# Three 256-wide matmuls per weight tile in one 256-wide PSUM region, and one VectorE pass per block

## The reference

```
a = rmsnorm(h);  proj = a @ w_in                       # 2048 x 6790
h = h + concat(hgrn2(proj), fox(proj), moba(proj)) @ w_out
c = rmsnorm(h);  h = h + (gelu(conv3(c @ w_gate)) * (c @ w_up)) @ w_down    # 5632 wide
e = rmsnorm(h);  h = h + sigmoid(e @ w_ple_gate) * (p @ w_ple_proj)
# second block; scale, shift and gates from silu(c_2) @ w_mod_2
h = mod(rmsnorm(x)); proj = h @ w_in_2                 # sliding-window heads and latent (MLA) heads
x = x + g1 * (mix @ w_out_2)
x = x + g2 * (relu(h @ w_ff1_2)**2 @ w_ff2_2)          # 8192 wide
out = rmsnorm(x)
```

## Time and profile before

| | |
|---|---|
| median of 3 runs | 2540.63 us (2538.52 to 2541.36) |
| profiled execution, first to last instruction | 2547.7 us |
| PE busy | 2419.6 us (95%), 13460 matmuls |
| PEld busy | 2057.7 us (81%) |
| DVE busy | 1946.2 us (76%), 3035 instructions |
| ACT busy | 1092.2 us (43%) |
| mean granted TensorE clock | 0.980 |
| HBM read | 509 MB, 202 GB/s over the span |

### The profile page before, as it was taken

The page is one execution under the profiler, slowest core; times in us unless marked ns, Lnnn a source line. Parts: engine busy times, 40 slices in busy tenths (PEclk is TensorE's granted clock), DMA queues, the critical chain, the costliest instruction groups (busy, mean ns, idle before and its releaser), DMA issues.

```text
span 2547.7 us, 37180 instructions
## 1 busy us (share of the span) xinstructions
PE 2419.6 (95%) x13460; PEld 2057.7 (81%) x13460; DVE 1946.2 (76%) x3035; ACT 1092.2 (43%) x1472; POOL 115.0 (5%) x221
## 2 busy tenths in 40 slices
PE   6979999989999999999988989899899999999997
PEld 5868787878888888888877867778788888888886
DVE  4688677779998989898976756676777777777775
ACT  4334444444434344444345444644444344334432
POOL 0100000000000000000000010000000000000000
PEclk8989999999999999999999989999999999999999
DMA  5754466357887878778864544334355555545552
GB/s 198 270 186 149 154 225 215 139 196 261 286 289 266 284 260 281 273 277 284 277 214 153 207 161 159 116 102 162 134 187 193 183 183 187 193 169 193 185 183 82
DMA packets 86666, 516.76 MB, mean 203 GB/s; under 512 B 9861, under 2 KB 10389, under 8 KB 37360
## 3 DMA queue, kind: packets, MB, share of 16 engines
q1 hardware_dynamic: 57168, 407.93, 44.8%
q0 software_dynamic: 29200, 106.31, 12.4%
q10 hardware_dynamic: 144, 0.26, 0.0%
HBM read 509.22 MB, written 5.24 MB: 202 GB/s over the span
## 4 chain that ended last, share of the span: by engine, by line
PE 86%; DVE 8%; ACT 3%; DMA 2%; issue 2%; SPq 0%; DVEq 0%; POOLq 0%; ACTq 0%
PE ps L464 47%; PE ps L465 24%; PE ps L462 5%; PE ps L461 2%; PE ps L482 2%; DMA modraw<-in_wmod 2%; PE ps L532 1%; DVE wl L1147 1%; DVE yn L1246 1%; ACT wh L776 1%; PE ps L541 1%; DVE modraw L1200 1%; PE ps L580 1%; DVE xs L1233 1%; PE ps L550 0%
## 5 line engine op out<-in xcount | busy, mean ns | idle before, releaser
L464 PE MATMUL ps<-xs,wh 128*128 128x512 f32 x4003 | 1462.6, 406 | 41.5 <-DVE xs L1233 17.3
L776 ACT ACTIVATE wh<-raw 128x1024 fp32r<-128x1024 f32 x768 | 809.9, 1058 | 1077.6 <-PE ps L462 810.1
L1147 DVE TENSOR_TENSOR wl<-raw,wh 128x1024 fp32r<-128x1024 f32 x768 | 937.3, 1222 | 317.7 <-ACT wh L776 301.6
L465 PE MATMUL ps<-xs,wl 128*128 128x256 f32 x4003 | 1131.5, 283 | 0.0
L464 PEld LDWEIGHTS ps<-xs,wh 128*128 128x128 f32 x4003 | 761.0, 190 | 242.4 <-issue 42.4
L465 PEld LDWEIGHTS ps<-xs,wl 128*128 128x128 f32 x4003 | 766.0, 191 | 11.3
L464 PE MATMUL ps<-hs,wh 128*128 128x512 f32 x1504 | 543.5, 400 | 5.7 <-DVE hs L1506 3.3
L465 PE MATMUL ps<-hs,wl 128*128 128x256 f32 x1504 | 423.1, 281 | 0.0
L464 PEld LDWEIGHTS ps<-hs,wh 128*128 128x128 f32 x1504 | 284.2, 189 | 65.4 <-DVE hs L1506 3.6
L465 PEld LDWEIGHTS ps<-hs,wl 128*128 128x128 f32 x1504 | 285.5, 190 | 10.0
L1200 DVE CUSTOM_DVE_ANT_0 modraw<-modraw,cb 128x1024 f32<-128x1024 f32 x192 | 233.4, 1218 | 24.8 <-DMA modraw<-in_wmod 24.6
(11 more groups left out here) (210 smaller groups left out, 1493.8 us busy)
## 6 DMA issues: line engine op xcount, KB each, us to landing
raw<-in_w SPq DMA_DIRECT2D x384, 1024.0 KB, 4.9
modraw<-in_wmod POOLq DMA_DIRECT2D x192, 512.0 KB, 4.3
rel_rows<-rrow POOLq DMA_DIRECT2D x4, 768.0 KB, 3.9
x<-in_x SPq DMA_DIRECT2D x4, 512.0 KB, 6.1
tbias<-rel_rows POOLq DMA_DIRECT2D x16, 128.0 KB, 2.8
out_dram<-mix SPq DMA_DIRECT2D x4, 512.0 KB, 2.6
hmask<-in_hmask SPq DMA_DIRECT2D x1, 512.0 KB, 17.3
mix<-in_p ACTq DMA_DIRECT2D x1, 256.0 KB, 4.2
```

Source lines behind the costliest of these rows:

```text
L464: nc.tensor.matmul(out[:, :], hi[:, w], pair, start=s, stop=e)
L465: m = nc.tensor.matmul(out[:, 0:T], lo[:, w], src[:, k, 0, :], start=False, stop=e, skip_group_check=e)
L776: nc.scalar.activation(wh[:, h % HS, :], raw[:, u % RAW, (h % 2) * 1024:(h % 2 + 1) * 1024], ACT.Copy).then_inc(s_round, 1)
L1147: nc.vector.tensor_tensor(wl[:, h % HS, :], raw[:, (h // 2) % RAW, (h % 2) * 1024:(h % 2 + 1) * 1024], wh[:, h % HS, :].bitcast(F32), ALU. ...
```

## The change

Every tile is now done as the joined units did it: three matmuls of 256 columns, hi·hi, hi·lo and lo·hi, all into columns 0 to 255 of the bank. The 512-column form, the turned order at the end of a block and the argument `joined` are gone. `take` becomes a copy of 256 columns, and `add_blocks` one instruction per block, without the `link` between two.

```
-                            pair = src[:, k, :, :].rearrange("p a t -> p (a t)")
-                            if joined:
-                                ...
-                            elif e and not s:
-                                nc.tensor.matmul(out[:, 0:T], lo[:, w], src[:, k, 0, :], start=False, stop=False)
-                                m = nc.tensor.matmul(out[:, :], hi[:, w], pair, start=False, stop=True)
-                            else:
-                                nc.tensor.matmul(out[:, :], hi[:, w], pair, start=s, stop=e)
-                                m = nc.tensor.matmul(out[:, 0:T], lo[:, w], src[:, k, 0, :], start=False,
-                                                     stop=e, skip_group_check=e)
+                            nc.tensor.matmul(out[:, 0:T], hi[:, w], src[:, k, 0, :], start=s, stop=False)
+                            nc.tensor.matmul(out[:, 0:T], hi[:, w], src[:, k, 1, :], start=False, stop=False)
+                            m = nc.tensor.matmul(out[:, 0:T], lo[:, w], src[:, k, 0, :], start=False, stop=e)
...
-                nc.vector.tensor_reduce(dst, bank()[:, :].rearrange("p (a t) -> p t a", a=2), AX.X, ALU.add
-                                        ).then_inc(s_evac, 1)
+                nc.vector.tensor_copy(dst, bank()[:, 0:T]).then_inc(s_evac, 1)
...
-                bs = [bank() for _ in ks]
-                for q in range(2):
-                    ...
-                    if q == 0:
-                        link(*ins)
+                for k in ks:
+                    b = bank()[:, 0:T]
+                    if gate is None:
+                        m = nc.vector.tensor_tensor(x[:, k, :], b, x[:, k, :], ALU.add)
                     else:
-                        for i in ins:
-                            i.then_inc(s_evac, 1)
+                        m = nc.vector.scalar_tensor_tensor(x[:, k, :], b, gate[:, k:k + 1], x[:, k, :], ALU.mult, ALU.add)
+                    m.then_inc(s_evac, 1)
```

More of the change, by code:

```diff
@@ L433, in _, with unit @@
             c = Counts(pe, h=0, b=0, hp=0)
-            def unit(kind, src, xwait=None, between=None, joined=False):
+            def unit(kind, src, xwait=None, between=None):
                 for half in range(2):
@@ L454, in unit @@
                             s, e = first and n == 0, last and n == len(tiles) - 1
-                            pair = src[:, k, :, :].rearrange("p a t -> p (a t)")
-                            if joined:
-                                nc.tensor.matmul(out[:, 0:T], hi[:, w], src[:, k, 0, :], start=s, stop=False)
-                                nc.tensor.matmul(out[:, 0:T], hi[:, w], src[:, k, 1, :], start=False, stop=False)
-                                m = nc.tensor.matmul(out[:, 0:T], lo[:, w], src[:, k, 0, :], start=False, stop=e)
-                            elif e and not s:
-                                nc.tensor.matmul(out[:, 0:T], lo[:, w], src[:, k, 0, :], start=False, stop=False)
-                                m = nc.tensor.matmul(out[:, :], hi[:, w], pair, start=False, stop=True)
-                            else:
-                                nc.tensor.matmul(out[:, :], hi[:, w], pair, start=s, stop=e)
-                                m = nc.tensor.matmul(out[:, 0:T], lo[:, w], src[:, k, 0, :], start=False,
-                                                     stop=e, skip_group_check=e)
+                            nc.tensor.matmul(out[:, 0:T], hi[:, w], src[:, k, 0, :], start=s, stop=False)
+                            nc.tensor.matmul(out[:, 0:T], hi[:, w], src[:, k, 1, :], start=False, stop=False)
+                            m = nc.tensor.matmul(out[:, 0:T], lo[:, w], src[:, k, 0, :], start=False, stop=e)
                     m.then_inc(s_used, 1)
@@ L680, in _ @@
             for j in range(U_PLEP):
-                unit("oct", xs, XS["p"] if j == 0 else None, joined=True)
+                unit("oct", xs, XS["p"] if j == 0 else None)
             square_sums(N_PLE, 2)
@@ L722, in _ @@
             for u in range(U_UQ):
-                unit("uq", xs, XS["cq"] if u == 0 else None, lambda q: swa(2 * (U_IN2 + u) + q), True)
+                unit("uq", xs, XS["cq"] if u == 0 else None, lambda q: swa(2 * (U_IN2 + u) + q))
             pe.wait_ge(s_xs, XS["cq"] + 4)
             for u in range(U_UKV):
-                unit("one", xs[:, 3:4, :, :], between=lambda q: swa(2 * (U_IN2 + U_UQ + u) + q), joined=True)
+                unit("one", xs[:, 3:4, :, :], between=lambda q: swa(2 * (U_IN2 + U_UQ + u) + q))
             def mla(i):
@@ L1170, in take @@
             def take(dst):
-                nc.vector.tensor_reduce(dst, bank()[:, :].rearrange("p (a t) -> p t a", a=2), AX.X, ALU.add
-                                        ).then_inc(s_evac, 1)
+                nc.vector.tensor_copy(dst, bank()[:, 0:T]).then_inc(s_evac, 1)
             def add_blocks(ks, gate=None):
-                bs = [bank() for _ in ks]
-                for q in range(2):
[L1179 to L1185, removed]
-                    if q == 0:
-                        link(*ins)
-                    else:
-                        for i in ins:
-                            i.then_inc(s_evac, 1)
+                for k in ks:
+                    b = bank()[:, 0:T]
+                    if gate is None:
+                        m = nc.vector.tensor_tensor(x[:, k, :], b, x[:, k, :], ALU.add)
+                    else:
+                        m = nc.vector.scalar_tensor_tensor(x[:, k, :], b, gate[:, k:k + 1], x[:, k, :], ALU.mult, ALU.add)
+                    m.then_inc(s_evac, 1)
             def mods(n, where=None):
@@ L1547, in _ @@
             MODS, M0 = 3 * CH, c.n["m"]
-            c.loop(NC1 - 1, ffn1_body, h=6 * CH, b=2 * CH + KB, c=KB + 2 * CH + 2, m=MODS, g=CH, y=CH, l=CH)
+            c.loop(NC1 - 1, ffn1_body, h=6 * CH, b=2 * CH + KB, c=2 * CH + 2, m=MODS, g=CH, y=CH, l=CH)
             units(CH_LAST, conv, first=lambda: product(CH - 1),
@@ L1667, in ffn2_body @@
                     units(CH, relu2, first=last_down(G2), h_lo_of=lambda j: h_lo(q, j))
-            c.loop(NC2 // 2 - 1, ffn2_body, h=8 * CH, b=2 * (CH + KB), c=2 * KB, y=2 * CH, l=2 * CH)
+            c.loop(NC2 // 2 - 1, ffn2_body, h=8 * CH, b=2 * (CH + KB), y=2 * CH, l=2 * CH)
             downs(lambda: relu2(CH - 1), lo_first=lambda: h_lo(1, CH - 1), gate=G2)
```

## The result

| | before | after |
|---|---|---|
| median | 2539.72 us (4 runs, 2538.52 to 2541.36) | 2610.42 us (4 runs, 2602.39 to 2612.8) |
| profiled execution, span | 2547.7 us | 2600.7 us |
| ratio of the runs | | 1.0273, 95% interval 1.0256 to 1.0289 |

The change costs 71 us; +34 was forecast, and the range ended at 2604. The two traces differ by only 53 us, because the profiled execution of before is longer than any of its four runs and that of after is the shortest of its four.

What follows compares the result with a forecast made beforehand. The prediction took the kernel to be bound by PE's stream of matmuls, priced by the distance between starts. Its terms, +42 (PE) - 1 (hidden) - 7 (DVE) = +34 us, gave 2575 us, range 2546 to 2604.

Steps and rivals of the forecast that it cites:

- PE, 120 ns a matmul, +42: PE's matmul stream: three 256-column matmuls at 120.0 ns replace a tile of about 353 ns, together +42 us.
- the end of the joined runs and not their beginning: Joined units: 120.0 ns a step from the ninth step on was taken, not 117.5 in the first 8 steps.
- The Trainium skill's rule on the busy share of LDWEIGHTS: PE's weight loads as the measure of headroom: would cost some 1300 us more; given no weight.
- The distance rule of N/2.4 + 2.5 ns: Distance between PE matmul starts: the third matmul would cost 2.5 ns a tile, +15 us; set aside against the rows.
- What hides, -1: From 70 to 145 us, some 12 full units: slower PE fills idle time while DVE is held by modulation weight loads, -1 us.
- Register operations in the loops, 0: Half boundaries of the two FFN loops, 384 halves: taken as nothing, upper bound 0.12 us each, +46 us.
- rival 3: FFN loop half boundaries become visible, 0.03 to 0.12 us each, +12 to +46: 2587 to 2621 us; chance 0.15.
- DVE, -7: DVE loses some 190 us of busy time, but only PE's waits count: -7 us, between 0 and -12.
- the two waits of L464 for `up`: PE waits counted among three for a take; those and four for `wl` save 0.27 each, 2 us.
- Sum, +34: Whole kernel: +42 - 1 - 7 = +34 us, giving 2575 us on the runs' median.
- Elsewhere in the stream nothing hides it: PE's stream outside 70 to 145 us: the slower matmul pace counts in full, with no further deduction.

Runs made afterwards that it cites:

- e6: Changed kernel with hi·lo put into columns 256 to 511, DVE's old eviction, and PE's FFN loops written out: 2576.44 us, ratio 1.0124 to the kernel before.
- e2: Kernel before with PE's two FFN loops written out, no jumps back: 2530.28 us, ratio 0.9959 to the kernel before.
- e4: Changed kernel with the middle matmul of each tile cut to 128 tokens: 2575.22 us in one run, clock 0.956.
- e8: Changed kernel with PE's FFN loops written out, second and third matmul of each tile cut to 128 tokens: 3865.97 us in one run, clock 0.587.
- e5: Kernel before's PE matmuls with FFN loops written out, DVE as in the changed kernel: 2527.91 us, ratio 0.9937 to the kernel before.
- e1: Changed kernel with PE's two FFN loops written out, no jumps back: 2567.08 us, ratio 1.0089 to the kernel before.
- e10: Changed kernel with PE's FFN loops written out, but twelve second-FFN units in a small loop of three rounds of four: 2568.69 us in one run.
- e9: Changed kernel with hi·lo in columns 256 to 511, DVE's old eviction, old matmul pair in first and last two units of each loop body: 2578.98 us.
- e3: Changed kernel with hi·lo put into columns 256 to 511 and DVE's old eviction, loops kept: 2607.77 us, ratio 1.0256 to the kernel before.
- e7: Changed kernel with hi·lo in columns 256 to 511, DVE's old eviction, old matmul pair in first two units of each loop body: 2595.59 us.

## Why the prediction was wrong

Point by point, by its own steps.

- *PE, 120 ns a matmul, +42.* Right: 0.120 us from start to start, 0.360 a tile, and +46 in e6 against e2. Taking the end of the joined runs and not their beginning was the right choice. The reason given, more time per column, was half of it: three pairs of load and matmul take 0.34 to 0.35 us a tile with 640 or 512 columns as well (e4, e8), and 0.36 is close to that floor.
- *The Trainium skill's rule on the busy share of LDWEIGHTS ("Perfetto Trace Analysis", Identifying the Most-Contended Engine).* Rightly set aside as a price: PEld is busy for all of a 100 us stretch after, against 87 before, and the pace changed by 2%. But it pointed at the right part of the engine: what lies 0.02 us under the tile's 0.36 is a floor of three load and matmul pairs. The distance rule of N/2.4 + 2.5 ns, which the prediction set beside it, is given by the Trainium skill ("TensorE: Matmul & The Clock Gate", Back-to-back issue gap) for an isolated matmul; for streams of load and matmul it has 131 ns at 512 columns, which these traces, with 235, do not bear out either.
- *What hides, -1.* Not resolved; the first FFN starts at 564.1 us before and 566.8 after, and at 557.8 in e2, whose code up to there is that of the kernel before.
- *Register operations in the loops, 0.* Right: halves in the loops are 2.88 us like those outside. (The middle of rival 3's 2587 to 2621 is 2604, as in the range, and not 2602.) Rival 3 put the loops' trouble at the wrong place, at each half and not at the jump.
- *DVE, -7.* Not contradicted (-2 to -6 in e5, -9 from e6 to e1). The copy lasts 0.42, not 0.41; there are 237 takes, not 221; busy time fell by 179 us, not 190. One term was misread: the two waits of L464 for `up`, counted as takes with 0.27 to save each, are jumps of the loops.
- *Sum, +34.* Right for kernels without jumps: +36.8.

The step that failed is a term that the sum +42 - 1 - 7 put at nothing without a reason: the jumps back of PE's two loops. "Elsewhere in the stream nothing hides it" took the stream as even, with 120 ns wherever no stage ends. It has five places where PE runs out of instructions. The trace before shows at each a gap of 1.0 to 2.7 us, which the forecast never looked at: three are the 3.8 us booked to issue, under several larger entries, and the other two stood in the earlier trace rows under DVE's name. What was measured in place of zero is +34 us, by the medians: 71 for the whole change, 37 for the same change without jumps.

The change makes a jump dearer in three ways that the traces show. The 17 matmuls already on their way last 1.9 us and not 2.8. In the second FFN the fetch now meets a weight load and waits for its end, 2.2 to 2.5 us more, and a second fetch does so again. And the granted clock falls to 1.2 GHz around four of the five jumps, for 3 to 10 us, where in the kernel before it fell at two, for 3 us each. Together the jumps went from some 10 or 14 to some 45 us, which is the missing half of the loss.

## What to carry to other kernels

On a bound TensorE, price a matmul form by the distance between starts in the same kernel, and count weight loads as well as columns: here, below 256 columns per load, narrower matmuls gained next to nothing. Then look at what each loop's jump back costs, since that price depends on how long the last matmuls before it take and on whether a large DMA has just begun when the branch is reached; a gap there may be booked to issue or to another engine; writing out a loop of a few thousand instructions, or keeping its body small, removes it. A forecast of a stream's pace is good to a few us only when the places where the stream breaks have been priced too.

## What the runs showed of the hardware

- PE's instruction stream arrives in transfers of 16 KB. After a branch back over a body of 1536 to 3072 loads and matmuls, PE starts 16 or 17 more matmuls and then waits, 3.7 to 6.4 us from the branch to the next one. A body of 384 loads and matmuls (e10) had no such wait and no transfer.
- In the second FFN the transfer started 1.0 us after the branch where the DMA queues were empty, and at the end of a 1 MB load, 3.2 to 3.6 us after it, where one had started with the branch (before and e9; after, e3 and e7; two jumps each). Of the changed kernel's 52 instruction transfers in that FFN none starts in the first 2.8 us of a load, though loads are under way for 58% of the time.
- A pair of a 128-column float32 weight load and a matmul takes some 113 to 116 ns at 2.4 GHz (e8, e4) and 213 at 1.2 (e8), where one or two of a tile's three matmuls have 128 columns.
- In e8 PE was busy for 98% of the span, and the same matmuls ran in stretches with a granted clock of 1.00 (2420 to 2550 us) and in stretches with 0.50 (900 to 1000 us); the mean was 0.587. What turns one into the other no run here shows.
